# Two merge projections in split precision, a later place for the attention's transposes, and upper banks for the first head

## What is computed

```python
# first block
h = rms_norm(x, g_norm); proj = h @ w_in
y_rwkv = (o_rwkv * silu(rwkv_gate)) @ w_proj_rwkv
...
y_conv = (u * silu(conv_gate)) @ w_proj_conv + b_proj_conv
...
y_mem = (att * silu(mem_gate)) @ w_proj_mem
y = gates[0] * y_rwkv + gates[1] * y_conv + gates[2] * y_mem
x = rms_norm(x + y @ w_out, g_final)
# second block, twice
h = rms_norm(x, norm_pre); proj = h @ w_in_2
y_a = gla_branch(...)      # gated linear scan, 4 heads
y_b = diff_branch(...)     # 4 heads: softmax(q1 k1) - lam * softmax(q2 k2), times v
y_c = hgrn_branch(...)     # gated linear scan, 4 heads
x = x + rms_norm(concat(y_a, y_b, y_c) @ w_out_2, norm_post)
```

## Time and profile before

| | before |
|---|---|
| median of 3 runs | 4360.05 us (4355.47 to 4360.43) |
| the profiled execution | 4344.91 us |
| its span, first to last instruction | 4343.1 us |
| mean granted TensorE clock | 0.949 |
| busy: PE, PEld | 3880.6 us (89%), 2368.6 us (55%) |
| busy: DVE, ACT, POOL | 1947.5 us (45%), 1516.2 us (35%), 957.3 us (22%) |
| chain that ended last, by engine | PE 69%, DVE 16%, ACT 10%, DMA 2%, POOL 2% |

### The profile page before, as it was taken

How to read it: one execution, slowest core, us unless ns; L and a number is a source line. 1 busy time by engine, 2 the same in 40 slices (tenths; PEclk the granted TensorE clock), 3 DMA queues, 4 the chain that set the end, 5 groups by cost and what they waited for, 6 DMA issues and landing times.

```text
span 4343.1 us, 66916 instructions
## 1 busy us (share of the span) xinstructions
PE 3880.6 (89%) x29404; PEld 2368.6 (55%) x29404; DVE 1947.5 (45%) x2101; ACT 1516.2 (35%) x1861; POOL 957.3 (22%) x426
## 2 busy tenths in 40 slices
PE   6988999999999999988999878988889888988887
PEld 3555666666666665446545445555554455555554
DVE  2556455654554653251303356244452246254552
ACT  4222223233232312241203343454463342454462
POOL 2413223342323322031113210110102200111102
PEclk9999999999999999999999987999999988999999
DMA  2111111111111112333211200000002100100002
GB/s 95 55 36 45 36 45 54 42 50 45 51 50 40 55 50 83 145 121 121 102 73 54 90 20 11 30 30 15 35 6 99 60 15 11 35 25 20 30 22 90
DMA packets 61586, 226.94 MB, mean 52 GB/s; under 512 B 6832, under 2 KB 8560, under 8 KB 60784
## 3 DMA queue, kind: packets, MB, share of 16 engines
q1 hardware_dynamic: 50064, 181.77, 11.9%
q10 hardware_dynamic: 11232, 40.90, 2.4%
HBM read 174.93 MB, written 47.71 MB: 51 GB/s over the span
## 4 chain that ended last, share of the span: by engine, by line
PE 69%; DVE 16%; ACT 10%; DMA 2%; POOL 2%; issue 1%; ACTq 0%; DVEq 0%; SPq 0%; POOLq 0%
PE psum L988 67%; DVE arena L2076 7%; ACT arena L1557 6%; DVE arena L2079 4%; DVE arena L2534 2%; ACT L1557 2%; PE psum L991 2%; DVE arena L2468 2%; ACT wh L1557 1%; DMA arena<-in_w_proj_conv 1%; POOL arena L2593 1%; DVE arena L2083 0%; POOL wl L2593 0%; ACT arena L2012 0%; DMA arena<-in_w_in 0%
## 5 line engine op out<-in xcount | busy, mean ns | idle before, releaser
L988 PE MATMUL psum<-arena 64*64 64x32 f32 (+11 forms) x19116 | 1563.3, 281 | 265.5 <-DVE arena L2076 94.6
L988 PEld LDWEIGHTS psum<-arena 64*64 64x64 f32 (+5 forms) x19116 | 1094.2, 157 | 764.1 <-issue 453.6
L988 PE MATMUL psum<-hh,wh 128*128 128x512 f32 x3120 | 885.3, 426 | 99.8 <-ACT hh L1557 25.9
L2593 POOL TENSOR_TENSOR wl<-arena,wh 128x1024 bf16<-128x1024 f32 (+1 forms) x195 | 472.3, 2422 | 2264.9 <-ACT wh L1557 2263.4
L1557 ACT ACTIVATE arena<-psum 128x512 f32<-128x512 f32 (+4 forms) x660 | 416.2, 631 | 1113.4 <-PE psum L988 816.6
L988 PE MATMUL psum<-hh,wl 128*128 128x512 bf16 x3120 | 791.3, 394 | 1.1 <-POOL wl L2593 1.1
L988 PEld LDWEIGHTS psum<-hh,wh 128*128 128x128 f32 x3120 | 589.2, 195 | 294.5 <-issue 56.9
L988 PE MATMUL psum<-hl,wh 128*128 128x512 bf16 x3120 | 742.3, 383 | 4.8 <-POOL hl L2593 4.8
L2076 DVE TENSOR_TENSOR arena<-psum,arena 128x512 f32<-128x512 f32 (+3 forms) x488 | 319.4, 654 | 939.3 <-PE psum L988 614.1
L2079 DVE SCALAR_TENSOR_TENSOR arena<-arena 128x1024 f32<-128x1024 f32 x356 | 564.7, 1586 | 184.9 <-ACT arena L1557 168.8
L2593 POOL TENSOR_TENSOR arena<-arena 128x1024 f32<-128x1024 f32 (+4 forms) x142 | 363.4, 2559 | 943.7 <-ACT arena L1557 499.6
(11 more groups left out here) (38 smaller groups left out, 788.9 us busy)
## 6 DMA issues: line engine op xcount, KB each, us to landing
arena<-in_w_in SPq DMA_DIRECT2D x161, 512.0 KB, 3.5
scr_g<-arena ACTq DMA_DIRECT2D x24, 512.0 KB, 2.6
arena<-scr_g SPq DMA_DIRECT2D x24, 512.0 KB, 4.4
arena<-in_w_out SPq DMA_DIRECT2D x24, 512.0 KB, 3.5
arena<-in_w_mem_kv SPq DMA_DIRECT2D x16, 512.0 KB, 3.6
scr_x<-arena SPq DMA_DIRECT2D x16, 512.0 KB, 3.6
arena<-scr_x SPq DMA_DIRECT2D x16, 512.0 KB, 6.8
arena<-in_x SPq DMA_DIRECT2D x8, 512.0 KB, 10.9
```

Source lines behind the costliest of these rows:

```text
L988: return pe.e.matmul(o, l, r, start=start, stop=stop)
L2593: return pool.seq.tensor_tensor(o, a, b, op)
```

## The change

It does four things.

1. Merges 0 and 2 use the split form. There are new inputs "o" and "a" for it: high and low parts of `BA` are made by `split` steps, for "o" ahead of merge 0 and from the last block to the first, for "a" ahead of merge 2. `("m", 0, 0)` and `("m", 2, 0)` are in `EARLY`; `plain` keeps only the memory's keys.
2. The `split` steps of "u" leave `conv_norm` and stand after merge 0, since "o" holds `HH` and `HL` until then. `conv_norm` is woven in with 1.3 steps per part of 12 matmuls instead of 0.62 per part of 2.
3. In `attend`, the transposes of the older block stand one double yield later, with `dr` ahead of them; `WT` comes behind `e1`; `dv` and `do` are each followed by one unit instead of two; the scan's tiles may use all banks for 8 of the 12 units instead of 6.
4. In `qk_ready`, the first head's projections and rotations take upper banks.

```diff
--- before.py
+++ after.py
@@ -568,7 +568,7 @@
     def merge(b, w, h):
         for ct in range(NT):
             fetch(f"g{b}", ct)
-            yield from P(("m", b, ct), A[w][ct], h, back=(b == 0), deep=4 if h else 2)
+            yield from P(("m", b, ct), A[w][ct], h, back=(b == 0), deep=4)
             do("merge", b, ct)
             grid_s.leave((f"g{b}", ct))
 
@@ -604,7 +604,6 @@
             if k > 1:
                 do("ugate", k - 2)
                 grid_s.leave(("cg", k - 2))
-                do("split", "u", k - 2)
         ps.leave(("usqs",))
         do("q_load", 1)
 
@@ -643,14 +642,20 @@
                         two(("matt", h, j), ("matt", h, j), UPPER)
                         grid_s.leave(("mg", 2 * h + j))
 
+    for k in range(7, -1, -1):
+        do("split", "o", k)
     ahead = Filler(conv_norm())
-    weave(merge(0, "w_proj_rwkv", None), (ahead, 0.62))
+    weave(merge(0, "w_proj_rwkv", "o"), (ahead, 1.3))
     ahead.finish()
+    for k in range(8):
+        do("split", "u", k)
     ahead = Filler(memory())
     weave(merge(1, "w_proj_conv", "u"), (ahead, 3.1))
     ahead.finish()
     do("x_load")
-    run(merge(2, "w_proj_mem", None))
+    for k in range(8):
+        do("split", "a", k)
+    run(merge(2, "w_proj_mem", "a"))
 
     def closing(tag, w, h):
 
@@ -788,11 +793,12 @@
 
     def qk_ready(L, h):
 
+        among = LOWER if h else UPPER
         for i in range(2):
             key = ("dqk", L, h, i)
-            yield from copied(P(key, A["w_in_2"][L][6 + 4 * i + h], f"p{L}", deep=1, share=0.25), key, "dq_copy", L, h, i, share=0.25)
+            yield from copied(P(key, A["w_in_2"][L][6 + 4 * i + h], f"p{L}", deep=1, share=0.25, among=among), key, "dq_copy", L, h, i, share=0.25)
             yield 0.25
-            held(("rope", L, h, i), ("rope", L, h, i))
+            held(("rope", L, h, i), ("rope", L, h, i), among)
             yield 0.25
             do("turned", L, h, i)
             ps.leave(("rope", L, h, i))
@@ -841,26 +847,24 @@
                 ps.leave(("ds", L, h, q, c))
             room["levels"] = ANY
             yield
+            yield
+            do("dr", L, h, q)
         if n:
             for g in range(2):
                 one(("dt", L, *last, g), ("dt", L, *last, g), UPPER)
-            yield
-            for g in range(2):
-                do("WT", L, *last, g)
-        if n < 32:
-            do("dr", L, h, q)
         yield
         if n < 32:
             do("e1", L, h, q)
-            if n == 0:
-                yield
+        if n:
+            for g in range(2):
+                do("WT", L, *last, g)
+        yield
+        room["levels"] = LOWER
         if n:
             one(("dv", L, *last), ("dv", L, *last), UPPER)
-        room["levels"] = LOWER
-        if n:
-            yield
+            yield True
             do("do", L, *last)
-            yield
+            yield True
 
 
     PACE = (0.62, 0.59, 0.555, 0.555)
@@ -969,10 +973,10 @@
 
 
 
-    PLAIN = {"m": lambda key: BA, "km": lambda key: MT}
-
-
-    EARLY = [("lo", 0), ("m", 1, 0), ("fin", 0)]
+    PLAIN = {"km": lambda key: MT}
+
+
+    EARLY = [("lo", 0), ("m", 0, 0), ("m", 1, 0), ("m", 2, 0), ("fin", 0)]
     EARLY += [("dvp", 0, 0), ("sv", 0, 0, 0), ("post0", 0), ("dvp", 1, 0), ("sv", 1, 0, 0), ("post1", 0)]
 
     def ready_h(tag, k):
@@ -997,7 +1001,7 @@
         def proj(key, first, last):
             if PROJ[key][1] is None:
                 return plain(key, first, last)
-            _, h, n, m, _ = PROJ[key]
+            _, h, n, m, back = PROJ[key]
             o = pair(("proj", key))[0:m, 0:n]
             i = 1024 * place_s[key]
             hi, low = wh[:, i:i + 8 * m], wl[:, i:i + 8 * m]
@@ -1011,34 +1015,30 @@
                 else:
                     kind, c0, k = q // each, q % each // 8 * 512, q % 8
                 c1 = min(n, c0 + 512)
+                begin, end, k = k == 0, k == 7, 7 - k if back else k
                 if kind == 0:
                     pe.wait_ge(*at("hi", h, k))
-                    x = mm(o[:, c0:c1], cols3(hi, 8)[:, k, :], HH[:, k, c0:c1], k == 0, False)
+                    x = mm(o[:, c0:c1], cols3(hi, 8)[:, k, :], HH[:, k, c0:c1], begin, False)
                 elif kind == 1:
                     pe.wait_ge(*at("w_lo", key))
                     x = mm(o[:, c0:c1], cols3(low, 8)[:, k, :], HB[:, k, c0:c1], False, False)
                 else:
                     pe.wait_ge(*ready_h(h, k))
-                    x = mm(o[:, c0:c1], top_half(hi, 8)[:, k, :], HL[:, k, c0:c1], False, k == 7)
+                    x = mm(o[:, c0:c1], top_half(hi, 8)[:, k, :], HL[:, k, c0:c1], False, end)
                 if q == 3 * each - 1:
                     x.then_inc(*pe.up("proj", key))
 
         def plain(key, first, last):
-            _, _, n, m, back = PROJ[key]
+            _, _, n, m, _ = PROJ[key]
             o = pair(("proj", key))[0:m, 0:n]
             if first == 0:
                 cleared(("proj", key))
                 pe.wait_ge(*at(f"w_in{place_w[key]}", key))
             for q in range(first, last):
                 c0, k = q // 8 * 512, q % 8
-                c1, k = min(n, c0 + 512), 7 - k if back else k
+                c1 = min(n, c0 + 512)
                 begin, end = q % 8 == 0, q % 8 == 7
-                if key[:2] == ("m", 0):
-                    pe.wait_ge(*(at(f"o{k}", "o", k) if k else at("o", 7)))
-                elif key[:2] == ("m", 2):
-                    pe.wait_ge(*at("att", 3, 1))
-                else:
-                    pe.wait_ge(*at("mem_norm"))
+                pe.wait_ge(*at("mem_norm"))
                 w3 = cols3(stage_w[place_w[key]][:, 0:8 * m], 8)
                 x = mm(o[:, c0:c1], w3[:, k, :], PLAIN[key[0]](key)[:, k, c0:c1], begin, end)
                 if q == (n + 511) // 512 * 8 - 1:
@@ -1504,7 +1504,7 @@
     for key_ in order:
         if PROJ[key_][1]:
             final[PROJ[key_][1]] = key_
-    HS_BEFORE = {"u": "h", "y": "u", "p0": "y", "m0": "p0", "p1": "m0", "m1": "p1"}
+    HS_BEFORE = {"o": "h", "u": "o", "a": "u", "y": "a", "p0": "y", "m0": "p0", "p1": "m0", "m1": "p1"}
 
     ROOT_FIN = stat_acc("pre0")
     EPS_ONES = sl(4096, 128)
@@ -1530,6 +1530,10 @@
             return [at("ugate", k)]
         if tag == "y":
             return [at("merge_pool", 2, k)]
+        if tag == "o":
+            return [at(f"o{k}", "o", k) if k else at("o", 7)]
+        if tag == "a":
+            return [at("att", k // 2, k % 2)]
         L = int(tag[1])
         if tag[0] == "p":
             return [at("norm_pre", L, k)]
```

## The result

The changed kernel takes 4382.47 us, median of 5 runs (4377.71 to 4389.25), beside 4355.47 us for the kernel before (5 runs, 4344.93 to 4360.43). The ratio is 1.007, interval 1.0055 to 1.0084: about 30 us **slower** (24 to 37), where 47 to 52 us of gain were forecast. The time lies outside the range of 4270 to 4340 us.

The account below looks back on a forecast made before the run. The prediction took TensorE, busy for 89% of the span, as the bound. Third merge -16, first merge -16, `w_out` step 0, turn -20 and upper banks 0 made -52 us: median near 4308 us, range 4270 to 4340.

Parts of the forecast that it names:

- Third merge, -16: Third merge split: first block 18.9 us, seven at 10.75, 94.2 instead of 110.0; -16 us, bounds -19 and -10.
- Step to `w_out`, 0: From third merge to `w_out`: y's conversion starts later but POOL still limits; 0 us, bounds 0 and +2.
- First merge, -16: First merge split, u's conversions moved: second quarter of first conv block near 1932.5, against 1948.46; -16 us, bounds -8 and -24.
- Its inputs first need high halves from ACT: Start of first merge: ACT free at 1805.5, first block ends near 1819.6, about 2 us later than now.
- about 1851: First merge: DVE finishes low halves, additions, mean and variance, merge products at about 1851, against 1855.0 now.
- third rival: First merge gives nothing because POOL's new work blocks DVE products in the normalisation's chain; -36, 4324 us; chance 0.12.
- 13 us, so 44.2 - 13 = 31 us remain: Gates' chain before the second merge: removing u's conversions takes out POOL's four low halves, 13 us, leaving 31.
- 5 us go back: Start of second merge: u's moved conversion delays the memory's keys on ACT and PE's third key block; 5 us lost.
- The turn, -20: Attention layers: later transposes lose most waits for the exponential; -10 per layer, -20 us, bounds -50 and +40.
- the copy of the transposes on ACT now comes behind the rescaling: Attention turn, cost of the new order: `WT` behind a rescaling of about 1.1 us, `dv` still four units after transposes.
- Upper banks, 0: Ramp into a layer: first head's queries and keys in upper banks; 0 us, bounds -8 and +4, both layers.
- The fourth: Rival, end of the turn: `qk` held back by `do` on ACT, +56 - 32 = +24, 4384 us; chance 0.07.

Follow-up runs that it names:

- e8: Kernel before with the third merge alone split and all low halves of a and y made by DVE: 4335.6 us, ratio 0.9958.
- e11: Kernel before with the change's merges alone, two weight loads of the first merge held until the second block of o has landed: 4352.1 us, ratio 0.9994.
- e14: Kernel before with the change's merges alone, all low halves of o, u, a, y by DVE and two first-merge weight loads held back: 4337.9 us, ratio 0.9959.
- e12: Kernel before with the change's merges alone and all low halves of o, u, a and y made by DVE: 4341.18 us, ratio 0.997.
- e18: Kernel before with third merge split, first plain, low halves of u, a, y by DVE, u's conversions moved behind the gates: 4330.01 us, ratio 0.9934.
- e2: Kernel before with the new order inside a turn of the attention (`attend`) alone: 4391.74 us, ratio 1.009.
- e9: Kernel before with the new turn alone, but the `WT` copies ahead of `e1` on ACT: 4372.05 us, ratio 1.0041.
- e7: Kernel before with the turn's short end alone (`dv`, `do` one unit each; scan's tiles all banks for 8 units), transposes unmoved: 4369.64 us, ratio 1.0038.
- e15: Kernel before with the older block's steps one unit later, that unit taken from between `WT` and `dv`, long end kept: 4407.15 us, ratio 1.012.
- e16: Kernel before with `e1` two units earlier, ahead of `WT` and straight behind the reciprocal, long end kept: 4422.48 us, ratio 1.015.
- e3: Kernel before with upper banks for the first head's queries and keys (`qk_ready`) alone: 4352.15 us, ratio 0.9998.
- e13: Kernel before with third merge split and low halves of u, a, y by DVE, u's still between the gates: 4353.05 us, ratio 0.9986.
- e5: Kernel before with the new turn alone, the scan's tiles allowed all banks for four units instead of eight: 4415.61 us, ratio 1.014.

## Why the prediction was wrong

**Third merge, -16: right.** 19.0 us for the first block (2197.05 to 2216.0, when DVE has it), 12.3 for the second, 10.72 for each of the other six against 10.75 forecast; 14.4 us in the profile, 11 timed alone. I had given the second block 10.75 too, though the block behind the twin's transition took 12 us already (2312.6 to 2324.6). POOL limits the first block as said; with DVE alone (e8) the merge is 1.1 us shorter, not 5, since eight low halves then take DVE 14.7 us.

**Step to `w_out`, 0: right.** DVE has its first block at 2311.54, 18.9 us after PE's end at 2292.6, as before.

**First merge, -16: wrong by 32 us.** The second quarter of the first conv block comes at 1964.87, 16.4 us later than in the earlier trace rows, instead of 16 earlier. The forecast that PE would be through earlier and the normalisation's chain with it did not hold. The steps that failed, in order, with what each adds to the 32:
- *"Its inputs first need high halves from ACT", from 1805.5 on: 7 us.* They start at 1812.74. 2.4 us of this come from further up and 4.5 us from the issue of the seven loads of `o`, 10.24 us instead of 5.75. In the same microseconds SyncE issues two more weight loads, since the split form's staging comes free at once; e11 and e14 shorten the issue to 6.6 and 6.8 us by holding these, but start it later, so that the merge as a whole gains little.
- *DVE through with mean and variance "about 1851": 15 us more.* It is through at 1873.03. The four low halves took 11.3 us, and five of the seven additions 2.5 instead of 1.3 each, some 8 us together. This is where the port rule, which I had weighed only in the third rival, stands in the chain. PE's wait for the first sum, 8.3 us, I had not foreseen at all, and DVE in turn waits 3.9 us for PE behind it; that way back wasn't in my addition of DVE's times. The wait for the sum of squares is 8.0 us, not 6. The memory's normalisation began at 1896.57, not near 1873, which is 1 us more. When DVE alone makes the low halves (e12), some 5 us of this come back, counted to the second quarter.
- *"13 us, so 44.2 - 13 = 31 us remain": 6 us.* The chain without `u` takes 37 us (first gating product 1900.78, weights asked for at 1937.94). e18 measures the move by itself: 9.9 us instead of 13. I took all of POOL's low halves out of the chain, though the chain of waits named POOL only where it came last. The rest is new on POOL in the changed kernel: a weight subtraction of the split first merge, 3.4 us, stands in the chain.
- *"5 us go back": right in kind, 3 us more,* 1 of them for the landing of the conv weights (6.49 us instead of 5.47). PE waits 5.4 us there for the copy on ACT, 3.4 in e18, and not "some 15 us": it has 12.7 us of work in the 18 us from its start on the second merge to the second quarter.

On the rule: "only the shared port pair causes contention, and it's an exclusive lock" (the Trainium skill, "SBUF — State Buffer", section Who interferes with whom). The trace leans its way: a POOL subtraction takes 2.4 us alone and 3.3 beside DVE products that take 1.2 alone. A strict turn about would make 3.6 of a pair; 3.3 are measured.

**The turn, -20: wrong by 59 us.** That the wait for the exponential goes was right, 19 to 3 us per layer. But *"which covers nearly all of these"* failed: the transposes wait 28.2 us in the first layer instead of 34.4, now for ACT's copies and DVE's predicated copy. PE's waits for the predicated copy at the other matmuls, 29.3 us and the largest for DVE, and 16.5 us for DVE's products are not in the earlier trace rows; my working had them only as the scan's "own chain", without a price. The step that failed worst is *"the copy of the transposes on ACT now comes behind the rescaling (about as long as a cast, 1.1 us), and `dv` comes four units after the transposes as before"*, with which I put its cost at nothing. There are two faults in it. A unit is a mean: fillers come in whole pieces, and in the turn shown only 2.54 us of PE's work lie between `dt` and `dv`, not 7.6. And ACT takes its work in order, so what stands ahead of `WT` counts with what it waits for, not with its own length: a filler's copy that waits for PE, or `e1`, which waits for DVE. `dv`'s waits rose by 13 and 12 us in the layers, most of what the exponential's fell by; the transposes' other waits and DVE's came on top, and perhaps the lower clock. In measured parts: 21 us for `WT` behind `e1` (e2 less e9), 16 for the short end (e7), 2 for the late place with this end (e9 less e7, not to be told from none), together the 39 of e2. This division holds for this order of the steps only: with the long end the same parts cost other amounts (e15, e16).

The bound of +20 per layer "over DVE and ACT" was of the right size (20.2 and 13.3), but I took 40% of the gain as the value without a row for the new waits.

**Upper banks, 0: right** (e3).

**The rivals.** The fourth gave 4384 us, and 4382 were measured, but this is chance: it has the merges' full gain, and `qk` held by `do` with 56 us. `qk` waits 8.4 us in the first layer, 0.4 of it for ACT, where it waited 10.7 and 2.5. What was right of it is the place: the short end costs (e7), as far as one profile tells in clock rather than in waits of `qk`. The third rival named a part of what took the first merge's gain, some 8 of 32 us. Its condition, that the hindrance falls into the chain, was met before the gates, where I had said that it fell outside. I gave these two 0.19 together, and no case had both at once.

## What to carry to other kernels

Before moving a step, write down for each engine what stands ahead of it in that engine's order and what that in turn waits for: in this kernel, two copies placed behind one operation that waits for another engine cost 21 us, and 64 where that operation also followed straight on the one that it waits for, while the wait that the move was meant to cover was replaced by others when it was gone. A distance counted in a planner's units holds only on average. And a conversion shared between DVE and POOL isn't half as long as one on DVE alone: with both operands in SBUF, the kernels with DVE alone were the faster (e8, e12), except inside a chain where DVE must wait for a third engine (e13).

## What the runs showed of the hardware

The price of DVE and POOL side by side: for eight low halves DVE alone takes 12.6 us in e12 and 10.5 in e14 (`o`, behind ACT's high halves), 11.7 in e18 (`u`), and 14.7 in e8 and e12 (`a`, where POOL makes an addition meanwhile). The two engines together need 12.3 to 13.1 us for four each. The sharing gains next to nothing, and DVE's additions in the first merge take 2.5 us instead of 1.3 beside it.

The clock can cost as much as the waits. The idle time of e2 and e5 in the second layer is equal within 1.5 us, yet PE's busy time differs by 15.5 us at granted clocks of 0.91 and 0.89. The changed kernel has 19 waits of PE over 3 us in the first layer, where there were 10, and a mean clock of 0.90 instead of 0.93; that the one causes the other is argued, not shown, and profiles of the unchanged turn have 0.91 and 0.92 there with 9 to 11 such waits. Single runs of one kernel differ by this as well: e18's fastest and slowest run, 4323.60 and 4344.44 us, have mean clocks of 0.949 and 0.943. What sets the fall isn't settled by these runs.
